# Early z, scaled keys made between the levels, and 24 instead of 19 dots placed in each core stage of the delta net

## The reference, cut to what matters

```python
ue = jnp.take(u, ib, axis=0)
act = gb * jax.nn.gelu(jnp.einsum('nd,nkd->nk', tb, ue))
ve = jnp.take(v, ib, axis=0)
return jnp.einsum('nk,nkd->nd', act, ve)
```

```python
a_mat = jnp.where(strict, beta[..., :, None] * kk * decay, 0.0) + jnp.eye(CHUNK)
u = triangular_solve(a_mat, beta[..., None] * v)
w = triangular_solve(a_mat, (beta * jnp.exp(gc))[..., None] * k)
k_end = k * jnp.exp(gc[..., -1:] - gc)[..., None]
v_new = uc - jnp.einsum('bhcd,bhdv->bhcv', wc, state)
state = dc[..., None, None] * state + jnp.einsum('bhcd,bhcv->bhdv', kd, v_new)
```

## Time and profile before

| | us |
|---|---|
| median of three runs | 1924.41 |
| lowest and highest of them | 1919.62, 1926.65 |
| the profiled execution | 1926.93 |
| its span (first to last instruction) | 1925.1 |

### The profile page before, as it was taken

The page is one execution under the profiler, slowest core; times in us unless marked ns, Lnnn a source line. Parts: engine busy times, 40 slices in busy tenths (PEclk is TensorE's granted clock), DMA queues, the critical chain, the costliest instruction groups (busy, mean ns, idle before and its releaser), DMA issues.

```text
span 1925.1 us, 25074 instructions
## 1 busy us (share of the span) xinstructions
PE 1511.7 (79%) x9204; PEld 881.1 (46%) x9204; DVE 1295.1 (67%) x3968; ACT 423.4 (22%) x1171; POOL 594.0 (31%) x551
## 2 busy tenths in 40 slices
PE   7999899776766979879889687997889875555555
PEld 7644675333213646645558265564556641111111
DVE  5767756868886777574445776667735579778665
ACT  1212201000002722632211264154121210000001
POOL 0011134444342322332222322232232244444441
PEclk9999889677668988998999898999999997877887
DMA  9887589999998986996999998699699999999995
GB/s 368 338 325 302 207 342 421 421 421 419 421 421 340 421 333 244 422 347 244 394 410 402 399 401 323 253 377 374 219 375 391 415 371 421 421 422 421 422 421 229
DMA packets 100267, 703.51 MB, mean 365 GB/s; under 512 B 15264, under 2 KB 15648, under 8 KB 16560
## 3 DMA queue, kind: packets, MB, share of 16 engines
q0 software_dynamic: 78336, 570.46, 73.6%
q1 hardware_dynamic: 21808, 131.45, 16.8%
HBM read 700.82 MB, written 1.05 MB: 365 GB/s over the span
## 4 chain that ended last, share of the span: by engine, by line
PE 41%; DMA 24%; DVE 15%; issue 5%; ACT 5%; POOL 0%; DVEq 0%; POOLq 0%; ACTq 0%
PE PS L1661 16%; DMA ub<-in_peer_uv,idx 9%; DMA vb<-in_peer_uv,idx 8%; PE PS L1811 4%; PE PS L2036 3%; PE PS L2012 3%; DMA mods<-in_peer_uv,idx 2%; DMA ring<-in_peer_uv,idx 2%; PE PS L1717 2%; DVE ub L1155 2%; DVE vb L1155 2%; PE PS L1993 2%; DMA ring<-in_gdn_z 2%; ACT ring L1485 1%; PE PS L1970 1%
## 5 line engine op out<-in xcount | busy, mean ns | idle before, releaser
L1661 PE MATMUL PS<-vb,z 128*64 128x512 f32 x816 | 319.4, 765 | 123.4 <-DVE z L1121 116.3
L1661 PE MATMUL PS<-ub,z 128*64 128x512 f32 x832 | 318.8, 748 | 118.3 <-DVE z L1121 118.3
L2073 POOL DMA_INDIRECT ub<-in_peer_uv,idx x208 | 240.9, 1158 | 488.1 <-PE PS L1661 418.4
L2073 POOL DMA_INDIRECT vb<-in_peer_uv,idx x204 | 221.0, 1083 | 478.3 <-PE PS L1661 428.6
L1372 ACT ACTIVATE tanhs<-cubed 128x2 f32<-128x2 f32 x256 | 51.9, 203 | 838.3 <-DVE cubed L1110 837.5
L1661 PEld LDWEIGHTS PS<-vb,z 128*64 128x64 f32 x816 | 73.6, 164 | 273.8 <-DVE z L1121 173.9
L1661 PEld LDWEIGHTS PS<-ub,z 128*64 128x64 f32 x832 | 74.3, 161 | 263.0 <-DVE z L1121 169.0
L1114 DVE SCALAR_TENSOR_TENSOR acts<-tanhs,gated_x 128x2 f32<-128x2 f32 x256 | 40.2, 157 | 177.1 <-ACT tanhs L1372 176.8
L1155 DVE CUSTOM_DVE_ANT_0 ub<-ub,h 128x1024 f32<-128x1024 f32 x104 | 127.2, 1223 | 43.4 <-DMA ub<-in_peer_uv,idx 42.6
L1661 PE MATMUL PS<-mods,z 128*64 128x512 f32 x208 | 128.5, 750 | 31.6 <-DVE z L1121 31.6
L1155 DVE CUSTOM_DVE_ANT_0 vb<-vb,h 128x1024 f32<-128x1024 f32 x102 | 124.7, 1223 | 35.2 <-DMA vb<-in_peer_uv,idx 34.5
(11 more groups left out here) (365 smaller groups left out, 2679.8 us busy)
## 6 DMA issues: line engine op xcount, KB each, us to landing
ring<-in_gdn_qkv SPq DMA_DIRECT2D x32, 1024.0 KB, 9.7
ring<-in_peer_wq SPq DMA_DIRECT2D x23, 1024.0 KB, 9.6
two_slots<-in_ada_wide POOLq DMA_DIRECT2D x20, 1024.0 KB, 6.0
ring<-in_gdn_z SPq DMA_DIRECT2D x16, 1024.0 KB, 9.4
ring<-in_gdn_w_out SPq DMA_DIRECT2D x16, 1024.0 KB, 9.7
ring<-in_gla_w_in SPq DMA_DIRECT2D x6, 2048.0 KB, 9.7
mods<-in_ada_wide POOLq DMA_DIRECT2D x11, 1024.0 KB, 6.7
ring<-in_ada_w SPq DMA_DIRECT2D x4, 2048.0 KB, 11.6
```

The costliest lines, as they stand in the source:

```text
L1661: last = pe.matmul(y[64 * g:64 * g + 64, e, :], z[:, i % 4, g, :], rows[:, D + e * 512:D + (e + 1) * 512], start=False, stop=False, skip_g ...
L2073: pool.indirect_dma_start(row_buffers[b], None, uv_rows, off).then_inc(row_landed[b].sem, 16)
```

## The change

Three things change. (1) The plan times of the dots in tiles 1 and 2 follow a table PACE: 24 dots in each of the two core stages (86 to 164 and 236 to 314 units), 18 before, 17 between and 45 behind them, instead of one every 4.06 units. (2) z of a pair is made ahead of the next odd dot and not behind it. (3) KB and KE have tiles of their own, and their transposes and scaled copies are moved in between Y and X of levels 1 to 4. To make room, the five tiles of the levels are packed next to each other; nothing is computed differently.

```diff
-            X, _, LT, Y, _, bv = (area[:, n * D:(n + 1) * D].rearrange("p (v n) -> p v n", n=P) for n in range(6))
+            X, _, LT, KB, KE, bv = (area[:, n * D:(n + 1) * D].rearrange("p (v n) -> p v n", n=P) for n in range(6))
...
-            Xb, XTb, LTb, Yb, MTb = (area[:, n * D:n * D + HH * CH].rearrange("p (v n) -> p v n", n=CH) for n in range(5))
+            Xb, Yb, XTb, MTb, LTb = (area[:, n * HH * CH:(n + 1) * HH * CH].rearrange("p (v n) -> p v n", n=CH) for n in range(5))
...
+            PACE = ((0.0, 0), (86.0, 18), (164.0, 42), (236.0, 59), (314.0, 83), (B, STRETCH))
 
             def dot_at(w, n):
-                return W_AT[w] + (W_AT[w + 1] - W_AT[w]) * (n + 1) / STRETCH
+
+                if w in (0, 3):
+                    return W_AT[w] + A * (n + 1) / STRETCH
+                (at, of), (to, upto) = next((a, b) for a, b in zip(PACE, PACE[1:]) if n + 1 <= b[1])
+                return W_AT[w] + at + (to - at) * (n + 1 - of) / (upto - of)
...
+            KEYS = (("KB", 0), ("KB", 1), ("KE", 0), ("KE", 1))
...
                         order += [(("Y", lv, gq), "D") for gq in range(2)]
+                        order += [(KEYS[lv - 1], "A")] if lv <= len(KEYS) else []
...
-                    order += [(("KB", gq), "A") for gq in range(2)] + [(("WT", gq), "A") for gq in range(2)] + [(("KE", gq), "A") for gq in range(2)]
+                    order += [(("WT", gq), "A") for gq in range(2)]
...
                                 yield dot_at(w, n)
+                                if g and n > 1:
+                                    spread_weight(i - 1, weighed)
...
                                     dotted = v_chain.next()
-                                    if n > 1:
-                                        spread_weight(i - 1, weighed)
                                     gelu_argument(i, dotted)
...
                                     yield core.at("KB", gq) + core.dt * 0.5
-                                    act.wait_ge(mm.sem, core.product("T", NL - 1, 1))
                                     act.wait_ge(mm.sem, core.product("KB", gq))
-                                    scaled(Y, core.ps("KB", gq), be, gq, True)
+                                    scaled(KB, core.ps("KB", gq), be, gq, True)
+                                for gq in range(2):
+                                    yield core.at("KE", gq) + core.dt * 0.5
+                                    act.wait_ge(mm.sem, core.product("KE", gq))
+                                    scaled(KE, core.ps("KE", gq), ekend, gq, True)
...
+                                    if lv <= len(KEYS):
+                                        yield core.at(*KEYS[lv - 1])
+                                        ps = into(KEYS[lv - 1])
+                                        for e in range(2):
+                                            last = pe.transpose(ps[:, e, :], qk[:, 4 + KEYS[lv - 1][1] * 2 + e, :], ident[:])
+                                        last.then_inc(mm.sem, 1)
...
-                                        last = pe.matmul(ps[:, v_, :], Y[r, v_, :], XTb[r, v_, :], start=True, stop=True)
+                                        last = pe.matmul(ps[:, v_, :], KB[r, v_, :], XTb[r, v_, :], start=True, stop=True)
...
-                                            last = pe.matmul(ps[:, e, :], Y[r, v_, :], X[r, v_, :], start=True, stop=True)
+                                            last = pe.matmul(ps[:, e, :], KE[r, v_, :], X[r, v_, :], start=True, stop=True)
```

More of the change, by code:

```diff
@@ L1550, in mixer @@
                                     done(act.activation(LT[:, :, r], wt, ACT.Copy, scale=-1.0))
-                                for gq in range(2):
-                                    yield core.at("KE", gq) + core.dt * 0.5
-                                    act.wait_ge(mm.sem, core.product("KE", gq))
-                                    scaled(Y, core.ps("KE", gq), ekend, gq, True)
                                 for jj in range(2):
@@ L1914, in mixer @@
                                         last.then_inc(mm.sem, 1)
-                                for gq in range(2):
-                                    yield core.at("KB", gq)
-                                    ps = into(("KB", gq))
-                                    for e in range(2):
-                                        last = pe.transpose(ps[:, e, :], qk[:, 4 + gq * 2 + e, :], ident[:])
-                                    last.then_inc(mm.sem, 1)
                                 for jj, r in enumerate(CHUNKS):
@@ L1927, in mixer @@
                                     for v_ in range(HH):
-                                        last = pe.matmul(ps[:, v_, :], Y[r, v_, :], XTb[r, v_, :], start=True, stop=True)
-                                    last.then_inc(mm.sem, 1)
-                                for gq in range(2):
-                                    yield core.at("KE", gq)
-                                    ps = into(("KE", gq))
-                                    for e in range(2):
-                                        last = pe.transpose(ps[:, e, :], qk[:, 4 + gq * 2 + e, :], ident[:])
+                                        last = pe.matmul(ps[:, v_, :], KB[r, v_, :], XTb[r, v_, :], start=True, stop=True)
                                     last.then_inc(mm.sem, 1)
```

## The result

The changed kernel took a median of 1912.44 us (1904.49 to 1926.62, 18 runs) against 1924.03 us (1916.32 to 1931.48, 18 runs) for the kernel before, run beside it: ratio 0.9947 [0.9923, 0.9971], 10 to 12 us less. The forecast was 1896 us. The sign was right and the time lies in the range, but well under half of the 28.8 us was there.

The account below looks back on a forecast made before the run. Transfers bind tile 3, the order of dependent products sets a core's length, and elsewhere both engines are near their limit. Outside -38.4, cores +9.6, routing +3, early z elsewhere -3: -28.8 us, so 1896 us, range 1868 to 1926.

Parts of the forecast that it names:

- The outside sum: Tiles 1 and 2 outside the cores: 20 dots fewer save 38.4 us (19 to 50); early z there saves 3.
- the forecast 4.1: Tail of each core: moved keys save 2.3 us of waiting for scaled copies and 1.8 us of transposes.
- Its own signs: Right: core lengths within 3 us, z waits well under 6. Wrong: cores of 90 us, TensorE and VectorE below 80%.
- the one at 1308: Core with a 14-step routing job beside its dots; its length was to stay within 7 us of before.
- its two prices, 2.50 and 1.73: Saving in us per dot less outside the cores: 2.50 where rows are awaited, 1.73 where both engines are near their limit.
- Part 2: Inside a core: five more dots lengthen the levels by 4.3 us, early z's own price 1.2, the first part 1.0.
- the idle time stays: Levels of a core: TensorE's remaining 2.4 us of idle time is kept, so they take 30.2 us, +2.2.
- the busy share stays: Levels of a core: TensorE only keeps its old share of 81%, so they take 34.4 us, +6.4.
- The rival that put added dots in the chain: Levels: added dots lie in the chain, +13.6 us per core, +16 in all, about 1940 us; chance 0.12.
- that wait ends: Levels: z made before the odd dot ends TensorE's 0.74 us wait in each level, four of them 3.0 us.
- The feared cover failure: Levels: a tanh may wait behind four scaled copies, 1.1 us in each of four levels, 4.4 per core; counted as nothing.
- The routing core: Core at 1308 us: denser dots draw nearly the whole routing job into its levels, so 3 us added to 2.4.

Follow-up runs that it names:

- z_and_keys: The changed kernel with the dots at their old places, so early z and moved keys without the placement: 1899.93 us, ratio 0.9863.
- early_z_only: The kernel before plus the early z alone, dots and keys at their old places: 1894.05 us, ratio 0.9834.
- place_only: The kernel before plus the table PACE alone, 24 dots per core, z late and keys in the tail: 1947.38 us, ratio 1.0120.
- no_moved_keys: The changed kernel with the scaled keys back in the tail, early z and placement kept: 1904.11 us, ratio 0.9907.
- half_matmuls: The kernel before with early z alone, expert matmuls of the second half of the output columns left out: 1868.91 us, ratio 0.9722.
- later execution: Second profile of the changed kernel, unedited, read as the profile after: 1909.49 us, ratio 0.9937; the first profiled execution took 1925.33 us.
- z at once: z directly behind acts, ahead of the level's masks and additions; on the kernel before, dots and keys at old places: 1888.78 us, ratio 0.9807.
- early_z_14: The kernel before with early z, keys late, and 14 dots per core instead of 19: 1920.36 us, ratio 0.9962.
- z_keys_lev9: The kernel before with early z and all four key groups in levels 1 to 4, 9 dots in the levels, 18 per core: 1914.65 us, ratio 0.9940.
- at_once_24: The kernel before with z directly behind acts and 24 dots per core, keys not moved: 1905.58 us, ratio 0.9905.

## Why the prediction was right in sign and wrong in size

**Right.** Transfers bind tiles 0 and 3: neither moved. The outside sum, -38.4 and -3: measured -38.9, with 21 dots fewer there by the trace. The moved keys free the tail: the wait for scaled copies is gone from the W products (in its place 0.8 us for an addition), and the tails are 133.2 us before and 119.8 after, 3.4 per core against the forecast 4.1. With the dots at their old places the keys alone shorten the tails by 4.1 (z_and_keys against early_z_only). DMA in the first two cores: 343 and 341 GB/s, "near 350"; in the others 317 and 293.

**Its own signs.** For "right": the stage behind the second core came 8 us shorter, but the first three cores missed their bound of 3 us (+3.8, +7.2, +4.8), the one at 1308 its 7 (+11.7), and the z waits stayed. For "wrong": the fourth core, 103.4 us long with TensorE busy 76% and VectorE 72%. Two small misreadings change little: the stage between the cores loses 0.7 dots by the plan and not 1.0, and about 421 GB/s stand in 14 of the 40 slices, not in half of them.

**The outside, in the order of the forecast.** The forecast put the placement first, -38.4, and early z on top, -3. Measured in that order, place_only has -33.7 outside (1.6 per dot where 1.92 was taken), and early z on top of it -3.7 (no_moved_keys). Taken the other way round, early z alone has -13.4 and the placement on top -24.0. The two take some of the same time away, so neither has a share of its own. Where early z stands, a dot less is worth 1.3 us, far below the 2.50 of a transfer, though relief of TensorE comes through by only a third there (half_matmuls). A dot more costs 1.8. That suggests that what a dot less is worth shrinks with each that goes; the forecast held its two prices, 2.50 and 1.73, for all of them.

**The step that failed: Part 2, what dots cost inside a core.** It forecast +2.4 us per core and +3 for the routing core, 12.6 in all; measured +27.5 (later execution), about 7 per core. The levels were to grow by 4.3 and 1.2; they grew by 7.4, 6.4, 7.9 and 9.8. On top of early z, which made them shorter by more than forecast, dots and keys were to add 7.3 us per core and added 12.4. The heads grew by 2.3 per core where 1.0 was counted; of these 9.4 us in sum early z alone, with no dot added, already has 7.0, and why stays open. The busy times it summed for the levels of the first two cores were right to 2.5 us. What failed is the way from busy time to length: it took the middle between "the idle time stays" and "the busy share stays", and the measured length lies above both. The levels are a loop of dependent steps through both engines, and the idle time in it is neither a fixed amount nor a share. This is the length of the first core's levels by what lies in them:

| dots in the levels | late z | early z | z at once |
|---|---|---|---|
| 6 | | 25.4 | |
| 8 | | 26.2 | |
| 9 | 28.7 | 25.9 | 25.4 |
| 11 | 38.0 | 30.6 | 29.8 |
| 8, with keys | | 30.0 | |
| 10, with keys | 37.4 | 31.2 | |
| 13, with keys | 44.6 | 36.1 | |

Below 9 dots nothing is won: with early z there is a floor between 25 and 26 us. Above the floor, two dots more, one pair, cost 4.7 us with early z and 9.3 with late z, where their work is 1.94 us on TensorE and at most 3.4 on VectorE. Of the 4.7, TensorE's work is 1.4, its waits for z grew by 2.0 (0.9 to 2.9), and 2.1 is one new wait of T for the mask of the last level, which VectorE makes behind a dot and a routing step; the wait for the additions went down by 0.8. In the rows with keys part of the growth is routing: the longer plan of the levels draws 4.0 us of VectorE's routing steps into those of the first and third core, where early_z_only has 1.1.

The second core's levels hold no routing step in any of these runs, and show more plainly what counts. There are five levels. First early_z_14, then early_z_only and no_moved_keys, the levels of the second core:

```profile
830.40:855.00 24.60, 21.42 (x481) 15.63 (x475) 18.41 (x54) 1.15 (x5) 6.38 (x7) 1.00 0.81 292
820.30:845.60 25.30, 24.77 (x495) 16.67 (x492) 23.49 (x70) 1.55 (x7) 11.48 (x11) 1.00 0.99 380
833.50:865.10 31.60, 26.52 (x503) 16.85 (x500) 24.67 (x72) 1.63 (x8) 13.16 (x13) 1.00 0.97 379
```

| second core, early z | expert pairs in the levels | dots | length |
|---|---|---|---|
| early_z_14 | 3 | 6 | 24.6 |
| early_z_only | 5 | 10 | 25.3 |
| no_moved_keys | 6 | 11 | 31.6 |
| z_keys_lev9, with keys | 4 | 8 | 28.9 |
| z_and_keys, with keys | 6 | 10 | 31.4 |
| changed kernel, with keys | 7 | 13 | 37.6 |

With three pairs TensorE is busy 21.4 and VectorE 18.4 of 24.6 us, so neither load makes this floor. Two pairs more, one for each level, cost only 0.7 us, and TensorE is then busy 98% of the time. The sixth costs 6.3 us (8.6 with late z and 3.3 with z at once, by place_only and at_once_24), of which 1.8 is work of TensorE and 4.6 new idle time. Why the step comes just there is not shown; with early z it is about one more round of the loop (5.3 us, below). The keys cost something by themselves, as the row with four pairs shows. So the prediction added two pairs to a part that, once z was early, had no room left for one.

The rival that put added dots in the chain at (2 x 1.68 + 1.94) = 5.3 us per pair was nearer, and its place was right. Its 13.6 us per core was too dear for the whole change. That place_only has +13.1 is luck in part: the rival's sum holds 4.4 us of copies and -4.1 of the tail, which place_only doesn't have, and they nearly cancel.

**Early z was under-estimated and over-relied on.** The forecast gave it 3.0 us per core in the levels and 3 us elsewhere, less 1.2 per core for its own price: about 10 us. Alone it gives 32: the levels are 18.1 us shorter in sum, the outside 13.4. The level's period shows it. Before, two pairs of neighbouring levels start at 704.71 and here:

```profile
710.80 0.64 PE L1661 MATMUL PS<-mods,z 128*64 128x512 f32 x1 [0.74 <-DVE z L1121]
```

6.1 us. With early z only:

```profile
698.68 0.28 DVE L1121 TENSOR_TENSOR z<-spot,acts 128x128 f32<-128x128 f32 x1
...
698.79 0.63 PE L1913 MATMUL PS<-ring 64*64 64x64 f32 x16
698.88 1.22 DVE L1157 CUSTOM_DVE_ANT_0 vb<-vb,h 128x1024 f32<-128x1024 f32 x1
...
699.36 0.64 PE L1661 MATMUL PS<-mods,z 128*64 128x512 f32 x1
...
704.64 1.94 PE L1661 MATMUL PS<-vb,z 128*64 128x512 f32 x8
```

5.3 us: z is ready while TensorE still has T (L1913), so the pair follows T with no idle time, and the odd dot of 1.22 us lies beside the pair. In the changed kernel (later execution) the loop is another:

```profile
697.09 0.63 PE L1926 MATMUL PS<-ring 64*64 64x64 f32 x16
...
697.81 0.08 DVE L1165 DVE_READ_ACCUMULATOR2_ANT dots<- 128x1 f32 x1
697.81 0.16 DVE L1122 SCALAR_TENSOR_TENSOR acts<-tanhs,gated_x 128x2 f32<-128x2 f32 x1
697.88 0.75 DVE L1303 TENSOR_TENSOR ring<-ring,PS 128x256 f32<-128x256 f32 x2
698.54 0.29 DVE L1129 TENSOR_TENSOR z<-spot,acts 128x128 f32<-128x128 f32 x1
698.74 1.22 DVE L1165 CUSTOM_DVE_ANT_0 vb<-vb,h 128x1024 f32<-128x1024 f32 x1
...
698.88 1.94 PE L1668 MATMUL PS<-ub,z 128*64 128x512 f32 x8 [1.16 <-DVE z L1129]
```

Denser dots moved z to a place behind the additions of the level, which wait for T and for the even dot. TensorE has finished T at 697.7 (697.09 + 0.63) and idles 1.16 us. The prediction said that with z ahead of the odd dot "that wait ends"; it had read one thing that z stood behind, the odd dot, and not the next one. Hence the z rows of 5.7, 6.3 and 11.9 us, against 1.3, 2.7 and 5.2 for the same cores in early_z_only. But z's place is not the whole of it: at_once_24, with the same placement and z directly behind acts, waits only 0.6 us for z in the first core's levels and still needs 29.8 us. There 2.4 us of idle time is T's wait for the last mask and 1.3 is for an addition.

**Moved keys: a gain in the tail, a larger loss in the levels.** The tail's 4.1 came almost whole. For the levels the forecast had counted 1.3 us of transposes, and for the copies nothing. By z_keys_lev9 they cost 3.7 us in the first core's levels, and with the names that they add they draw 1 dot and, in two of the cores, 3 us of routing steps into them as well; in sum they cost 6 us of the whole time with early z and 12 without. The feared cover failure, a tanh behind the copies, is not what shows: the waits that grew are TensorE's for the mask.

**The routing core** was given 2.4 + 3 and took 11.7. Its levels hold 15.4 us of routing steps after the change and 7.6 before, 7.8 more where the forecast counted 6.5.

## What to carry to other kernels

Where two engines hand work to each other in turn, add up the period of one round along the hand-overs, with all that stands ahead of each step in its engine's order; busy time over an old share doesn't give a length; here a pair with 1.94 us of TensorE's work lengthened the loop by 4.7 to 6.3, once every round had its pair. Filler work has a price on both sides of its border and both change as it moves (0.6 to 1.8 us inside, 1.3 to 1.8 outside): measure a step in each direction before moving five. Take a bundle of edits apart: of this one, the two-line part alone was worth 32 us and the whole about 11.

## What the hardware showed that was not expected

In the first profiled execution TensorE's granted clock was at its lower level, 1.2 GHz, for 31 us on end while the engine was busy throughout. Table by stage, then two rows of TensorE's timeline, of that execution:

```profile
689.10:724.00 34.90, 27.61 (x494) 17.16 (x488) 29.91 (x102) 6.18 (x23) 16.33 (x14) 1.00 0.99 387
724.00:755.00 31.00, 30.51 (x150) 22.66 (x152) 19.13 (x66) 4.06 (x9) 4.36 (x4) 0.51 0.54 202
...
724.49 1.12 PE L1926 MATMUL PS<-ring 64*64 64x64 f32 x16 [2.04 <-DVE ring L1296]
725.53 3.68 PE L1668 MATMUL PS<-ub,z 128*64 128x512 f32 x8
```

Ahead of it the clock was 1.00 with TensorE busy 27.6 of 34.9 us, and the clock fell while the engine was idle for 2.04 us. The pair took 3.68 us instead of 1.94. The later execution of the same program has the same 2.04 us of idle time at the same place, ahead of 722.26 us, and keeps the clock there. It falls only at 728 us, and for 6.7 us:

```profile
722.26 0.68 PE L1926 MATMUL PS<-ring 64*64 64x64 f32 x16 [2.04 <-DVE ring L1296]
722.88 1.94 PE L1668 MATMUL PS<-ub,z 128*64 128x512 f32 x8
...
728.10:734.80 6.70, 6.70 (x49) 6.47 (x47) 4.16 (x14) 2.03 (x5) 0.00 (x0) 0.50 0.74 280
```

So that wait alone doesn't decide it, and what does stays open. The tails differ by 9.4 us, 38.2 against 28.8. The clock may also be behind the wider spread of the changed kernel's runs, 22 us against 15 of the kernel before: of its 18 runs, the nine below 1912 us have a mean granted clock of 0.868 to 0.881, the seven above 1916 us one of 0.856 to 0.866. Time and clock go together there; that the clock is the cause is not shown.
